# An attention step less beside the first rotary query panel, and a weight panel's low part two tiles later in the second norm

## The reference

```
proj = x @ w_in                       # q_a k_a v_a | q_b k_b v_b | g
o_a = chunked_relbias_attention(q_a, k_a, v_a, rel_bias)        # 8 heads of 64
o_b = differential_attention(rope(q_b), rope(k_b), v_b, lam)    # 4 heads, two maps each
merged = sigmoid(g_a) * (o_a @ w_branch_a) + sigmoid(g_b) * (o_b @ w_branch_b)
x = layer_norm(ALPHA * x + merged @ w_out, ln1_g, ln1_b)
x = layer_norm(ALPHA * x + square(relu(x @ w_ff1)) @ w_ff2, ln2_g, ln2_b)
x = hybrid_layer(x, ...)              # begins with proj = rmsnorm(x) @ w_in_2
out = rmsnorm(x, final_norm_w)
```

## Time and profile before

| what | value |
|---|---|
| median of 3 runs | 1449.7 us (1449.32 to 1449.98) |
| profiled execution | 1449.33 us, its span 1447.5 us |
| TensorE busy | 1419.6 us (98%) |
| VectorE, ScalarE, GpSimd busy | 817.4 (56%), 610.7 (42%), 134.3 us (9%) |
| TensorE clock granted, mean | 0.997 of 2.4 GHz |
| chain that ended last, TensorE's share | 89% |

### The profile page before, as it was taken

How to read it: one execution, slowest core, us unless ns; L and a number is a source line. 1 busy time by engine, 2 the same in 40 slices (tenths; PEclk the granted TensorE clock), 3 DMA queues, 4 the chain that set the end, 5 groups by cost and what they waited for, 6 DMA issues and landing times.

```text
span 1447.5 us, 19982 instructions
## 1 busy us (share of the span) xinstructions
PE 1419.6 (98%) x7898; PEld 1134.1 (78%) x7898; DVE 817.4 (56%) x1394; ACT 610.7 (42%) x1104; POOL 134.3 (9%) x116
## 2 busy tenths in 40 slices
PE   8999999999999999999999999999999999999997
PEld 6777777788788888888877777776778888888886
DVE  4545555557674343443468767676555763664463
ACT  4544455542363231322335755344444432342234
POOL 0000000012200000000012000440020210110012
PEclk9999999999999999999999999999999999999999
DMA  7222222113223223222233221110222232222221
GB/s 254 83 82 85 87 81 73 59 59 131 88 74 116 87 102 103 87 102 89 101 106 131 88 73 59 64 42 1 103 103 85 105 106 99 90 100 102 85 66 68
DMA packets 40348, 130.92 MB, mean 90 GB/s; under 512 B 4800, under 2 KB 5184, under 8 KB 40256
## 3 DMA queue, kind: packets, MB, share of 16 engines
q1 hardware_dynamic: 39392, 128.08, 25.5%
q10 hardware_dynamic: 864, 1.57, 0.3%
HBM read 124.92 MB, written 4.19 MB: 89 GB/s over the span
## 4 chain that ended last, share of the span: by engine, by line
PE 89%; DVE 5%; ACT 3%; issue 2%; DMA 1%; POOL 0%; SPq 0%; POOLq 0%; DVEq 0%; ACTq 0%
PE bank L1254 86%; PE bank L1257 3%; ACT Fm L1637 2%; DVE Fm L2091 1%; DVE Fm L1986 1%; DVE Wlo L1986 1%; ACT Whi L1637 1%; DVE Fm L1994 1%; POOL Fm L2570 0%; DVE Xf L1986 0%; DMA Fm<-in_relb_dram 0%; DMA Fm<-in_x_dram 0%; SPq L2665 0%; DVE sm L1990 0%; POOL Xf L2570 0%
## 5 line engine op out<-in xcount | busy, mean ns | idle before, releaser
L1254 PE MATMUL bank<-Rm,Whi 128*128 128x512 f32 x2816 | 872.7, 391 | 9.0 <-ACT Whi L1637 5.7
L1254 PEld LDWEIGHTS bank<-Rm,Whi 128*128 128x128 f32 x2816 | 529.8, 188 | 120.4 <-ACT Whi L1637 5.7
L1254 PE MATMUL bank<-Rm,Wlo 128*128 128x512 f32 x1408 | 563.2, 400 | 1.5 <-issue 1.3
L1986 DVE TENSOR_TENSOR Wlo<-Wraw,Whi 128x1024 fp32r<-128x1024 f32 (+2 forms) x225 | 283.9, 1265 | 143.1 <-ACT Whi L1637 142.5
L1254 PEld LDWEIGHTS bank<-Rm,Wlo 128*128 128x128 f32 x1408 | 265.2, 188 | 62.6 <-issue 8.2
L1637 ACT ACTIVATE Whi<-Wraw 128x1024 fp32r<-128x1024 f32 (+2 forms) x225 | 232.5, 1038 | 191.8 <-PE bank L1254 186.2
L1254 PE MATMUL bank<-Xr,Whi 128*128 128x512 f32 x736 | 226.8, 389 | 0.0
L2570 POOL TENSOR_TENSOR Fm<-Fm 128x512 f32<-128x512 f32 (+1 forms) x86 | 112.8, 1320 | 775.9 <-ACT Fm L1637 483.0
L1254 PEld LDWEIGHTS bank<-Xr,Whi 128*128 128x128 f32 x736 | 138.1, 188 | 28.7
L1637 ACT ACTIVATE Fm<-bank 128x512 f32<-128x512 f32 (+4 forms) x200 | 92.6, 483 | 150.0 <-PE bank L1254 103.0
L1986 DVE TENSOR_TENSOR Fm<-Fm,bank 128x512 f32<-128x512 f32 (+2 forms) x118 | 76.0, 664 | 121.9 <-PE bank L1254 121.7
(11 more groups left out here) (100 smaller groups left out, 712.4 us busy)
## 6 DMA issues: line engine op xcount, KB each, us to landing
Wraw<-in_w_in_dram SPq DMA_DIRECT2D x67, 512.0 KB, 3.3
Wraw<-in_w_ff_dram SPq DMA_DIRECT2D x64, 512.0 KB, 3.2
Wraw<-in_w_up_dram SPq DMA_DIRECT2D x44, 512.0 KB, 3.2
Wraw<-in_w_o_dram SPq DMA_DIRECT2D x16, 512.0 KB, 3.3
Wraw<-in_w_down_dram SPq DMA_DIRECT2D x16, 512.0 KB, 3.2
Wraw<-in_w_ab_dram SPq DMA_DIRECT2D x8, 512.0 KB, 3.3
Wraw<-in_w_down_end_dram SPq DMA_DIRECT2D x8, 384.0 KB, 2.9
Fm<-in_relb_dram SPq DMA_DIRECT2D x8, 256.0 KB, 3.9
```

Source lines behind the costliest of these rows:

```text
L1254: return e.matmul(o, l, r, start=first, stop=last)
L1986: return e.tensor_tensor(o, x, y, op)
```

## The change

Two numbers of the order change; no instruction is added or removed. The first rotary query panel (panel 12, u = 4) runs one attention step and not two, so each later step comes one slot later. In `layer_norm`, `low_weights()` keeps its place at i = 4 in the first norm and goes to i = 6 in the second, while `ready_weights` stays at i = 4 in both.

```diff
     for u in range(4, 8):
-        q = project("w_in", 8 + u, STEPS_B)
+        q = project("w_in", 8 + u, STEPS_B if u > 4 else STEPS_A)
         do("ropein", q)
...
             if i == 4:
                 ready_weights(st["taken"] + HL)
+            if i == (4 if norm == 0 else 6):
                 low_weights()
```

## The result

| what | before | with the change |
|---|---|---|
| median of 4 executions | 1449.8 us | 1471.7 us (1469.91 to 1474.33) |
| ratio to before | | 1.0144, 95% interval 1.013 to 1.0158 |
| profiled execution | 1449.33, span 1447.5 | 1474.33, span 1472.5 |
| granted clock, mean of the span | 0.997 | 0.991 |

The change costs 22 us. The forecast was slower, 1465 with a range of 1456 to 1470.5; the median lies 1.2 us outside the range, in the case that the prediction called "TensorE's clock falls too" (1468 to 1473) and gave 0.12.

What follows compares the result with a forecast made beforehand. The prediction took TensorE to be the bound and counted only its waits: 1449.3 us profiled, plus 15.3 for the first edit and 0.45 for the second, gave 1465 us, with a range of 1456 to 1470.

Steps and rivals of the forecast that it cites:

- TensorE's clock falls too: Rival: new waits of 2 to 3 us may each lose up to 1.7 us at half clock; 1468 to 1473, chance 0.12.
- the first edit: Attention steps one slot later from panel 12 to the end of the gates: 7.2 + 5.8 + 2.35 = 15.3 us.
- The strips: Units 2 and 3: strips issued behind swaps and a load make first masks late, 2.85 us each; old waits go, -1.75.
- The turns behind them: Turns of value panels 17 and 20 wait for ScalarE's late copy: 2.15 us and 1.1 us.
- Under the gates: Units 4 to 7: turns wait for a copy and VectorE's mix; +1.75 per unit, three times +5.2, unit 4 +0.6.
- The last unit: After unit 7's last values, TensorE has 12 matmuls instead of 24 to cover the scaling: +2.35 us.
- The second edit: Second norm: 1.3 us wait at tile 5 becomes 2 us at tile 7, GpSimd's adds interleaving; net +0.45 us.

Runs made afterwards that it cites:

- the filled execution: The first edit alone plus three and four unused matmuls where TensorE waits for strips 2 and 3: 1468.75 us (1.0136); repeated 1471.0 (1.0145).
- the first edit alone: Kernel before with only panel 12 cut to one attention step, second norm as before: 1471.9 us (1.0131); repeated 1470.9 (1.0144).
- The step given back at the first gate: The first edit alone, with the lost attention step run in the first gate panel (three steps there): 1461.3 us (1.0061).
- Giving the step back late: The first edit alone, with the lost attention step run in the last gate panel but one (three steps there): 1467.0 us (1.0115).
- the adds' experiment: The second edit alone, with the squares and GpSimd's adds of tiles 5 to 7 moved behind the norm's tile loop: 1450.4 us (0.9995).
- the low part behind tile 7: The second edit alone, but the fourth panel's low part placed after tile 7 instead of between tiles 6 and 7: 1450.7 us (1.0002).
- the second edit alone: Kernel before with only the second norm's low part moved from i = 4 to i = 6: 1452.0 us (1.0009).

## Why the prediction was right and wrong

The forecast for the first edit was 15.3 us without the clock. Without the clock it is 17.9 in the filled execution and, by the estimate above, some 16.7 with the strips of the change's own profile.

**The strips.** Right in kind, too small. SyncE issued strip 2 at 122.23 (I said 120.8) and strip 3 at 159.64 (157.5), each behind four swaps and a load. The waits were 3.2 and 3.5 us with the change, 3.1 and 4.4 with the first edit alone, 3.6 and 4.5 where they were filled (from the row before to the scores), for 2.85 each. From the first swap to the mask it was 8.17 us for strip 2, as computed from strip 3 of before (8.1), but 8.5 for strip 3: its second DMA took 4.13 us and not 3.74, and some 5 in the first edit alone (issued near 160.9, masked from 166.01 on), with a panel's load issued 0.1 us behind it. That is 1.0 us too little for the change's profile and 2.4 for the filled one.

**The turns behind them.** Right in place. Value panel 17: 2.15 forecast, 1.7 with the clock at 1.00; panel 20: 1.1 forecast, 0.85. With the slow clock ahead, 0.9 and nothing.

**Under the gates.** Right in total, less so in the parts. By the panels' ends of the two traces (10.04, 11.47, 13.12, 14.79 us behind at the same place of four units in a row) unit 4 costs 1.43 and the next two 1.65 and 1.67, for 0.6 and 1.75 forecast. Unit 4 waits for its mix like the others, which the sum had not. Within a unit the copy holds TensorE for 0.21 and not 0.9, the mix for 1.07 as forecast (with its restart 1.2 for 1.3) and the score banks for 0.35: that the total of a unit is so near is in part luck. The step given back at the first gate shows that the order makes these waits.

**The last unit.** 2.4 measured (2.24 and a restart), 2.35 forecast. Giving the step back late removes it, and a wait of 1.5 for a copy comes in its place.

**The second edit.** +0.47 in the trace for +0.45 forecast, with the duration of the low part as computed; the adds' experiment shows the reason.

**The step that failed** is the clock, which the sum put at nothing and the rivals set apart with 0.12: "Against: after the 1.14 us wait in the norm it stayed at 1.00, and much of a slow stretch would lie in a later wait." The first half drew from a wait of 1.14 to waits of 3. In the attention stretch the clock stayed at 1.00 behind the waits of 1.1 to 1.5 here too; behind those of 2.2 to 4.3 it fell at 12 places of 16 in the eight profiles that have such waits. (It stayed behind one wait of 3.2 for strip 2, and behind the last unit's 2.2 in the three profiles whose strips were early or filled.) The second half was right in part at the strips, where 5.1 us by name cost 2.6, and wrong for the other two falls: of 1.7 by name 1.5 and 1.6 were seen at the panels' ends, since no wait followed. That the clock had been slow once before is not so either: it fell at the end of the span too (0.70 from 1440 to 1450).

Added up for the profile of the change: 15.3 forecast, 1.4 more of waits, 4.1 of clock in the attention, then 0.5 and a fall of 1.6 for the second edit. Without the clock the kernel would be near 1449.3 + 16.7 + 0.5 = 1466.5 us (an estimate), inside the range. Over the executions it is the same picture: the rest grew by 14 to 15 us, from 1446.4 to 1447.4 up to 1461.6, and the clock's part by name by 5 to 7, from 2.9 to 5.2 up to 10.3.

## What to carry to other kernels

A new standstill of TensorE is worth more than its length. Here the clock fell behind 12 of 16 waits of 2.2 to 4.3 us, so count a stretch at half clock behind such a wait as the likely case, in full where no other wait follows (1.5 of 1.7 us) and in part where one does (2.6 of 5.1). In a queue that issues strictly in turn, look what a moved transfer is moved behind: two pairs of DMAs, moved behind swaps that wait for a copy, carried 13 to 14 of the 22 us. Where executions of one kernel differ by several us, separate the clock's share from the rest before reading a difference of 2 us.

## What was not expected of the hardware

The same wait at the same place is followed by a slow stretch in one execution and not in another: behind the wait for strip 2, 3.10 us with the change (0.88 and 0.95 granted in the next two stretches), 3.20 us with the step given back (1.00 and 1.00), and two stretches at 0.83 with the first edit alone. The slow stretch begins with the restart or up to 1.2 us behind it (behind the last unit's scaling TensorE restarted at 324.38 and its matmuls became slow at 325.56) and cost 1.7 or 3.4 us. Shorter standstills were followed by it as well. With the low part behind tile 7, waits of 0.7 and 0.9 us stand 1 us apart, and the stretch from 770 to 780 was granted 0.76. Behind a wait of 1.7 us in the decay stage, which every profile has, the clock fell in two of 15. And it fell at the head of the second norm, with no wait above 0.2 us ahead of it, in five of 15. What decides was not found; the filled strips show only that with the standstills cut to 0.9 and 1.1 us none came there. The Trainium skill ("TensorE: Matmul & The Clock Gate", Part 1) says that the gate judges TensorE's recent activity by a clock of its own, which doesn't start with the kernel, so that one program meets it at another phase each time; the spread over executions agrees (1.4 to 10.2 us of clock in twelve executions of the second edit alone), but no run here isolates it.
